# Layer norms of a two-layer hybrid kernel: squares summed with the tokens on partitions

## The reference

```python
def layer_norm(x, g, b):
    xf = x.astype(jnp.float32)
    mu = jnp.mean(xf, -1, keepdims=True)
    var = jnp.mean(jnp.square(xf - mu), -1, keepdims=True)
    return ((xf - mu) * lax.rsqrt(var + LN_EPS)).astype(x.dtype) * g + b

xl = layer_norm(DN_ALPHA * xl + ml[2] * mix_l, ln1_g[l], ln1_b[l])
h = jnp.concatenate([xc * (1 + mc[4]) + mc[3], xl * (1 + ml[4]) + ml[3]], axis=1)
f = channel_mixer(h, l, ...)
xl = layer_norm(DN_ALPHA * xl + ml[5] * f_l, ln2_g[l], ln2_b[l])
```

## Time and profile before

| | |
|---|---|
| runs | 2729.87, 2723.61, 2729.55 us; median 2729.55 us |
| profiled execution | 2728.8 us |
| its span in the trace | 2727.1 us |
| PE busy | 2483.1 us (91%) |
| PE weight loads busy | 1550.7 us (57%) |
| DVE busy | 780.7 us (29%) |
| ACT busy | 636.2 us (23%) |
| POOL busy | 589.7 us (22%) |
| mean granted TensorE clock | 0.96 of full |

### The profile page before, as it was taken

One profiled execution on the slowest core, in us unless ns is written; L12 is line 12 of the kernel. 1 busy time (PEld: TensorE's weight loads), 2 busy tenths in 40 slices (PEclk: granted clock), 3 DMA queues, 4 the chain that ended last, 5 costly groups with the idle time before them and its releaser, 6 DMA issues.

```text
span 2727.1 us, 63124 instructions
## 1 busy us (share of the span) xinstructions
PE 2483.1 (91%) x28806; PEld 1550.7 (57%) x28806; DVE 780.7 (29%) x1430; ACT 636.2 (23%) x971; POOL 589.7 (22%) x361
## 2 busy tenths in 40 slices
PE   5997799779999999696898799999999999999997
PEld 3674577457777778484676644444444444344444
DVE  2125666542222223517565410100000010101002
ACT  1232554332222222343654200000000000000002
POOL 4332543323344434245442200000000000000000
PEclk8999899889999999898999899999999999999998
DMA  7451000213434442130002489999898989898990
GB/s 249 152 173 47 6 4 4 93 62 138 155 139 156 147 160 93 47 101 8 7 4 65 194 320 352 355 354 358 342 368 324 384 329 381 330 370 335 375 359 29
DMA packets 197130, 536.49 MB, mean 197 GB/s; under 512 B 6640, under 2 KB 80640, under 8 KB 191744
## 3 DMA queue, kind: packets, MB, share of 16 engines
q1 hardware_dynamic: 193728, 528.50, 52.5%
q10 hardware_dynamic: 3136, 3.85, 0.4%
HBM read 531.28 MB, written 1.05 MB: 195 GB/s over the span
## 4 chain that ended last, share of the span: by engine, by line
PE 47%; DVE 2%; issue 1%; ACT 1%; POOL 0%; DMA 0%; POOLq 0%; DVEq 0%; ACTq 0%; SPq 0%
PE bank L719 24%; PE bank L722 12%; PE bank L692 1%; PE bank L750 1%; PE bank L707 1%; PE bank L710 1%; PE bank L1717 1%; PE bank L1713 1%; PE bank L1728 1%; PE bank L1690 0%; POOL w_lo L306 0%; PE bank L1613 0%; PE bank L1699 0%; ACT arena L1065 0%; DVE arena L1487 0%
## 5 line engine op out<-in xcount | busy, mean ns | idle before, releaser
L719 PE MATMUL bank<-arena 128*32 128x512 f32 (+1 forms) x6624 | 814.1, 559 | 20.9 <-issue 19.6
L722 PE MATMUL bank<-arena 128*32 128x256 f32 (+1 forms) x6624 | 488.7, 362 | 0.0
L306 POOL TENSOR_TENSOR w_lo<-arena,w_hi 128x2048 fp32r<-128x2048 f32 x78 | 354.6, 4547 | 591.1 <-ACT w_hi L300 591.1
L722 PEld LDWEIGHTS bank<-arena 128*32 128x32 f32 x6624 | 220.0, 110 | 435.6 <-issue 407.5
L316 PE MATMUL bank<-h_hi,w_hi 128*128 128x512 f32 (+1 forms) x1008 | 388.1, 385 | 49.7 <-DVE h_lo L1221 40.9
L318 PE MATMUL bank<-h_hi,w_lo 128*128 128x512 f32 (+1 forms) x1008 | 376.3, 373 | 0.0
L317 PE MATMUL bank<-h_lo,w_hi 128*128 128x512 f32 (+1 forms) x1008 | 373.8, 371 | 0.0
L719 PEld LDWEIGHTS bank<-arena 128*32 128x32 f32 x6624 | 210.4, 110 | 144.5 <-issue 36.2
L316 PEld LDWEIGHTS bank<-h_hi,w_hi 128*128 128x128 f32 x1008 | 192.7, 191 | 116.7 <-issue 61.2
L634 DVE TENSOR_TENSOR arena<-arena,bank 128x768 f32<-128x768 f32 (+2 forms) x45 | 31.3, 713 | 696.1 <-ACT arena L509 696.1
L318 PEld LDWEIGHTS bank<-h_hi,w_lo 128*128 128x128 f32 x1008 | 192.1, 191 | 35.8
(11 more groups left out here) (263 smaller groups left out, 2591.3 us busy)
## 6 DMA issues: line engine op xcount, KB each, us to landing
arena<-in_moe_w_dram SPq DMA_DIRECT2D x189, 2048.0 KB, 9.5
arena<-in_w_mod_dram SPq DMA_DIRECT2D x48, 1024.0 KB, 5.0
arena<-in_ffn_w_dram SPq DMA_DIRECT2D x42, 1024.0 KB, 7.1
arena<-in_w_in_dram SPq DMA_DIRECT2D x26, 1024.0 KB, 5.5
arena<-in_w_out_dram SPq DMA_DIRECT2D x8, 1024.0 KB, 9.4
arena<-in_ctx_dram ACTq DMA_DIRECT2D x1, 1024.0 KB, 11.3
arena<-in_x_dram ACTq DMA_DIRECT2D x1, 1024.0 KB, 13.3
arena<-in_w_in_dram SPq DMA_DIRECT2D x2, 512.0 KB, 5.1
```

The costliest lines, as they stand in the source:

```text
L306: pool.tensor_tensor(lo, slot_view(splits[i][0]), hi, ALU.subtract).then_inc(sem("w_lo"), 1)
L719: mm(bank[b][64 * h + 32 * c:64 * h + 32 * c + 32, 0:n // 2], xa[:, 32 * c:32 * c + 32], w[:, n // 2 * h:n // 2 * (h + 1)], start=first, s ...
L722: ins = mm(bank[b + 1][blk(q), 0:n // 4], xb, w[:, n // 4 * q:n // 4 * (q + 1)], start=first, stop=last)
```

## The change

The squares now stand as the stationary operand, a block of 128 tokens at a time, and the moving operand is one column of `mean_w`. The result is a column of 128 numbers: the variance of 128 tokens, with the tokens on the partitions. For 512 tokens that gives four columns in bank 5 (two for 256), summed over the eight `k`. Epsilon, root and reciprocal act on these 128x4 (or 128x2) numbers in a small new tensor `dev`. To bring the result back to all partitions in the layout of `X`, PE multiplies a stationary operand in which the column is repeated 128 times with the identity, once for each 128 tokens, into bank 4, which held the mean. The multiplication of the blocks reads bank 4 where it read `RSTD` in SBUF. PE waits for the reciprocal (`ln_inv`) and for the mean to be read (`ln_d`), DVE for these products (`ln_rows`).

```diff
+        dev = sb("dev", [P, L, 2, NT])
...
+        def dev_of(n, tok):
+
+            return dev[:, n // 2, n % 2, tok.start // P:tok.stop // P]
...
-                act.activation(RSTD[:, tok], RSTD[:, tok], ACT.Sqrt).then_inc(sem("ln_std"), 1)
+                act.activation(dev_of(n, tok), dev_of(n, tok), ACT.Sqrt).then_inc(sem("ln_std"), 1)
...
-                nc.vector.tensor_scalar(RSTD[:, tok], bank[5][:, tok], LN_EPS, None, ALU.add).then_inc(sem("ln_ve"), 1)
+                nc.vector.tensor_scalar(dev_of(n, tok), bank[5][:, tok.start // P:tok.stop // P], LN_EPS, None, ALU.add) \
+                  .then_inc(sem("ln_ve"), 1)
                 dve.wait_ge(sem("ln_std"), n + 1)
-                link(nc.vector.reciprocal(RSTD[:, tok], RSTD[:, tok]))
+                nc.vector.reciprocal(dev_of(n, tok), dev_of(n, tok)).then_inc(sem("ln_inv"), 1)
+                dve.wait_ge(sem("ln_rows"), n + 1)
                 wait(dve, "ln_sq", KD * (n + 1))
                 for k in range(KD):
-                    nc.vector.tensor_tensor(X[:, k, tok], X[:, k, tok], RSTD[:, tok], ALU.mult).then_inc(sem("ln_norm"), 1)
+                    nc.vector.tensor_tensor(X[:, k, tok], X[:, k, tok], bank[4][:, tok], ALU.mult).then_inc(sem("ln_norm"), 1)
...
                 for k in range(KD):
                     pe.wait_ge(sem("ln_sq"), KD * n + k + 1)
-                    mm(bank[5][:, tok], mean_w[:], SQ[:, k % 2, tok], start=(k == 0), stop=(k == KD - 1)) \
-                        .then_inc(sem("ln_vmm"), 1)
+                    for t in range(tok.start // P, tok.stop // P):
+                        ins = mm(bank[5][:, t:t + 1], SQ[:, k % 2, t * P:(t + 1) * P], mean_w[:, 0:1],
+                                 start=(k == 0 and t == tok.start // P), stop=(k == KD - 1), skip_group_check=True)
+                    ins.then_inc(sem("ln_vmm"), 1)
+                pe.wait_ge(sem("ln_inv"), n + 1)
+                pe.wait_ge(sem("ln_d"), KD * (n + 1))
+                for t in range(tok.start // P, tok.stop // P):
+                    ins = mm(bank[4][:, t * P:(t + 1) * P], dev[:, n // 2, n % 2, t:t + 1].to_broadcast([P, P]), ident,
+                             start=True, stop=True)
+                ins.then_inc(sem("ln_rows"), 1)
```

## The result

| | before | changed |
|---|---|---|
| median of 22 runs | 2729.12 us | 2734.39 us |
| lowest | 2721.32 us | 2725.78 us |
| profiled execution, its span | 2728.8, 2727.1 us | 2730.28, 2728.5 us |
| PE busy, DVE busy | 2483.1, 780.7 us | 2499.3, 767.9 us |

The ratio is 1.0024, with a 95% interval of 1.0015 to 1.0033: 6.5 us slower, 4.1 to 9.0. (One run of the changed kernel took 9297.65 us and one of the kernel before 2769.83 us; the ratio is taken without them, and the medians hardly move.) The forecast was 2732, no change that can be told, with a loss of 3.0 us behind it.

What follows compares the result with a forecast made beforehand. PE, busy 91% of the span, was taken to bound the kernel, with every norm step on its path. Early norms 2 x (4.05 - 2.2) plus late 2 x (0.7 - 1.05) lose 3.0 us on 2728.8: 2732, range 2722 to 2739.

Steps and rivals of the forecast that it cites:

- The norms are on the path: At all four norms: each step lies on the path, so what a norm gains or loses is the kernel's.
- What goes, and the small operations: Behind each sum: epsilon, root, reciprocal, 4.78 us early and 2.76 late, go; small ones with gaps take 0.65.
- The products with the identity: Behind the reciprocal: eight pairs early, four late, at half clock, 1.70 and 0.85 us, plus about 0.2 drain.
- the rival on the held clock: In the norms: clock stays full, 9.9 us gained, 2719; fourth norm's root waits some 0.4 us for its table; chance 0.12.
- The sum of squares: In each norm: clock falls 3.9 us after the mean's last wide product; 4.0 and 4.1 us lost early, 0.7 each late.
- The rival with the clock down from the start: In each norm's sum: all eight blocks at half clock, 9.1 us lost in all, 2738; chance 0.12.
- The total: Whole kernel: 2 x (4.05 - 2.2) + 2 x (0.7 - 1.05) = 3.0 us lost.
- the sum by that rule: Early norm's sum of squares by the LDWEIGHTS section: 6.8 us for 64 loads at either clock, a gain.

Runs made afterwards that it cites:

- The old sum with the new steps: Changed kernel with the sum of squares of the kernel before (mean_w stationary, 512 tokens moving), nine expert-loop turns fixed; ratio 1.0038 to the kernel before.
- small operations only: Kernel before with epsilon, root and reciprocal on four elements a partition, no product added, nine expert-loop turns fixed; ratio 0.9971 to the kernel before.
- the second profile: Changed kernel run again with no edit, for another profile; ratio 1.0023 to the kernel before, profiled execution 2730.71 us.
- the filling: Kernel with 128 moving columns plus unread 384-column products behind the identity products of the first three norms; ratio 0.9977 to the kernel before.

## Why the prediction was right

**The norms are on the path.** Kernels whose norms shrink get faster by most of it: -7.7 in the norms and -6.5 us (3.0 to 10.4) in the ratio; -11.0 and -9.3 (5.2 to 13.4); -12.1 and -7.9. The old sum with the new steps is the exception: -8.15 in the norms and slower in the whole, by its loop. Whether a part of the gain is lost in the loop with the others too, these intervals do not tell. The profiles hint at it: up to the start of the fourth norm's mean the stretch of the loop took 1157.2 to 1159.6 us with the four kernels of shorter norms, and 1154.0 to 1156.1 in the profile before and the two of the change; the half clock held there for 36.1 to 45.4 us and for 33.5 to 39.9 us.

**What goes, and the small operations.** Right. 0.16, 0.20 and 0.17 to 0.18 us, and 0.65 us from epsilon to multiplication where no product stands between them (small operations only), as reckoned.

**The products with the identity.** The step said 2.55 us from epsilon to multiplication in the early norms and 1.7 in the late ones. Measured 2.77 and 2.78, 1.90; in the fourth 2.25 and 1.91. They came at the half clock, as assumed; the drain and the hop to DVE were mis-sized by 0.2 us. 2.25 is the fourth norm of the first profile: there the clock held almost to the end of the sum, and the root at 2715.01 had to wait for its table, as the rival on the held clock had it for that norm (0.4 us).

**The sum of squares.** The mechanism was right: pairs at 0.11 us as long as the clock is up, 0.21 after, and the clock falls under them as if PE stood idle. After the end of the mean's products it fell after 4.7, 2.9, 4.7 and 5.3 us in the first profile, and 2.2, 3.4, 3.5 and 2.1 in the second, mean 3.6; I had counted 3.9, from the falls behind idleness before. The rival with the clock down from the start came near in two of the eight sums, where it fell 0.8 and 1.2 us behind the first product of squares. The early sums, to the epsilon, were said to be 11.7 us and are 10.98, 12.50, 13.17 and 12.21; the late ones 5.65, and are 5.30, 4.69, 5.77 and 6.49. That their mean comes within 0.1 us of the forecast is partly luck, as the single ones differ by 1.8 us.

**The total.** 3.0 us of loss was said; the norms of the two profiles lost 2.75 and 6.59, mean 4.7, and the runs 6.5 (4.1 to 9.0). So the size was low by a factor near two: it is a difference of two larger terms, the sum's loss (9.5 us forecast) and the steps' gain (6.5). Against the terms of the prediction the mean of the two profiles has 0.2 to 0.4 us less gained at each norm's steps, 1.0 us in all, and 0.7 us more lost in the four sums of squares, with a fall 0.3 us earlier than counted. That leads from 3.0 to the norms' 4.7. The 1.8 us from there to the runs' 6.5 no profile places; they lie inside the interval. Behind the first norm and outside the others the two profiles differ from before by -1.7 to +1.5 us a stretch, in sum by -1.0 and +0.7, so no cost shows there in both. The range, 2722 to 2739, held 2734.4.

**The rules of the Trainium skill.** In the Trainium skill "TensorE: Matmul & The Clock Gate" says in its section on why this matters for your kernels to keep TensorE busy without gaps for the full clock; a PE busy for 7.13 of 7.13 us at 0.50 speaks against it as long as the work is narrow. By its LDWEIGHTS section a load of 128 columns takes an estimated 0.107 us, which is what the pairs show at the full clock (0.11) and half of what they show at the half clock (0.21); the sum by that rule, a gain, did not come.

## What to carry to other kernels

Turning a matmul round so that the data is stationary and one column moves does not save PE's time: each 128 columns of data cost a weight load (two in this fp32 program), and the clock may fall to half although PE never pauses. Before shrinking the moving operand, look in the trace for a stretch of narrow products and read its granted clock; moving 128 columns in place of one cost nothing here (a record every 0.11 us either way at the full clock) and kept 2.4 GHz. Small reductions on [128 x few] do pay (4.78 us became 1.86 at the full clock), if the two halves of such a change are timed apart.

## What the runs showed of the hardware

- Work of 128 columns was done faster than work of one: 64 pairs in 7.87 us against 10.94 and 13.13.
- The granted clock fell from 1.0 to 0.5 in nine stretches of narrow products (eight sums, and the router's products behind the filling), 2.1 to 5.3 us after the last wide product in the eight sums. In eight of the nine PE was busy all through the 0.25 us in which it fell; in the fourth norm of the second profile it was busy for 0.13 of them.
- The kernel before spread over 18 us with no edit (2718.9 to 2737.3 us in 33 runs). The time goes with the mean granted clock of the run: 0.963 in the fastest and 0.955 in the slowest, and over the 33 runs the two have a correlation of -0.90. In the changed kernel the moment of the clock's fall moved the first norm's sum from 10.94 to 13.13 us. A single profile shows one draw of it.
